# A three-block transformer kernel: forgetting sums apart from the decays, 64 rows a head, and another order of work around the SSD loop

## The reference, cut to what matters

```python
u = rmsnorm(x, norm_mix)
(pool_v, q, k, v, f_logit, z, xbc, dt_raw, gate_logits) = split_columns(u @ w_in)
y_pool = pool_mixer(pool_v, ...) @ p_pool
# forgetting attention, 8 heads of 64
c = cumsum(log_sigmoid(f_logit + f_bias))                 # one row a head
s = q @ k.T * scale + (c[query] - c[key]), causal
y_attn = (softmax(s) @ v) @ p_attn
# SSD, 16 heads of 64, 2 groups, 4 chunks of 128 tokens
xbc = silu(causal_dwconv(xbc)); dt = softplus(dt_raw + bias); a = dt * A
a_cs = cumsum(a) in each chunk
y = (C B^T * exp(a_cs[l] - a_cs[s])) @ (x * dt)  +  exp(a_cs) * C @ state
y = (y + d_skip * x) * silu(z); rms norm in groups of 512 channels, * norm_w
y_ssd = y @ p_ssd
gates = sigmoid(gate_logits)
x = x + (gates[0] * y_pool + gates[1] * y_attn + gates[2] * y_ssd) @ w_out
```

## Time and profile before

| | us |
|---|---|
| median of 3 runs | 2301.11 |
| lowest and highest | 2300.15, 2301.57 |
| the profiled execution | 2300.4 |
| its span on the core | 2298.6 |
| PE busy | 2221.3 (97%) |
| DVE busy | 1391.9 (61%) |
| ACT busy | 795.7 (35%) |
| mean granted clock of PE | 0.988 |

### The profile page before, as it was taken

The page is one execution under the profiler, slowest core; times in us unless marked ns, Lnnn a source line. Parts: engine busy times, 40 slices in busy tenths (PEclk is TensorE's granted clock), DMA queues, the critical chain, the costliest instruction groups (busy, mean ns, idle before and its releaser), DMA issues.

```text
span 2298.6 us, 28503 instructions
## 1 busy us (share of the span) xinstructions
PE 2221.3 (97%) x10128; PEld 1756.8 (76%) x10128; DVE 1391.9 (61%) x2100; ACT 795.7 (35%) x1161; POOL 0.2 (0%) x4
## 2 busy tenths in 40 slices
PE   7999999999999999999999999989899999999998
PEld 5777688888886666788888867777678888888886
DVE  5666654554447776655454475577754557888744
ACT  4445432222225554322222223446622323222222
POOL 0000000000000000000000000000000000000000
PEclk9999999999999999999999999999999999999999
DMA  4111133333331111233333322222223332333332
GB/s 128 55 55 55 46 92 101 91 100 90 99 96 56 55 55 46 78 96 99 96 96 95 100 66 65 53 59 65 55 81 103 92 98 87 99 100 93 94 101 87
DMA packets 368642, 188.29 MB, mean 82 GB/s; under 512 B 8968, under 2 KB 368313, under 8 KB 368569
## 3 DMA queue, kind: packets, MB, share of 16 engines
q1 hardware_dynamic: 368569, 187.30, 28.5%
HBM read 185.18 MB, written 2.10 MB: 81 GB/s over the span
## 4 chain that ended last, share of the span: by engine, by line
PE 83%; DVE 10%; ACT 4%; issue 3%; DMA 0%; DVEq 0%; SPq 0%; ACTq 0%
PE lin L1548 73%; PE S L1572 1%; DVE dmax L992 1%; PE ob L1603 1%; ACT w_hi L520 1%; PE S L1585 1%; DVE conv L1256 1%; PE ob L1697 1%; DVE w_lo L877 1%; PE S L1811 1%; PE S L1590 1%; PE S L1575 1%; DVE prob L1005 0%; PE ob L1837 0%; DVE q_raw L1014 0%
## 5 line engine op out<-in xcount | busy, mean ns | idle before, releaser
L520 ACT ACTIVATE w_hi<-raw 128x1024 fp32r<-128x1024 f32 x361 | 381.0, 1056 | 825.4 <-PE lin L1548 817.3
L877 DVE TENSOR_TENSOR w_lo<-raw,w_hi 128x1024 fp32r<-128x1024 f32 x361 | 441.0, 1222 | 207.4 <-ACT w_hi L520 206.5
L1548 PE MATMUL lin<-h_hi,w_hi 128*128 128x512 f32 x1928 | 498.1, 400 | 7.4 <-DVE exact L1435 2.8
L1548 PE MATMUL lin<-h_lo,w_hi 128*128 128x512 f32 x1928 | 480.5, 391 | 0.0
L1548 PE MATMUL lin<-h_hi,w_lo 128*128 128x512 f32 x1928 | 478.3, 390 | 0.0
L1548 PEld LDWEIGHTS lin<-h_hi,w_hi 128*128 128x128 f32 x1928 | 362.3, 190 | 95.4 <-issue 14.1
L1548 PEld LDWEIGHTS lin<-h_hi,w_lo 128*128 128x128 f32 x1928 | 360.9, 188 | 74.8 <-issue 0.5
L1548 PEld LDWEIGHTS lin<-h_lo,w_hi 128*128 128x128 f32 x1928 | 360.2, 188 | 74.8 <-issue 0.8
L1548 PE MATMUL lin<-gu_lo,w_hi 128*128 128x512 f32 x528 | 131.4, 389 | 0.0
L1548 PE MATMUL lin<-gu_hi,w_lo 128*128 128x512 f32 x528 | 131.4, 389 | 0.0
L1548 PE MATMUL lin<-gu_hi,w_hi 128*128 128x512 f32 x528 | 131.4, 389 | 0.0
(11 more groups left out here) (311 smaller groups left out, 2241.8 us busy)
## 6 DMA issues: line engine op xcount, KB each, us to landing
raw<-in_w_in_dram SPq DMA_DIRECT2D x108, 512.0 KB, 3.8
raw<-in_w_gate_dram SPq DMA_DIRECT2D x44, 512.0 KB, 3.7
raw<-in_w_up_dram SPq DMA_DIRECT2D x44, 512.0 KB, 3.8
raw<-in_ffn_up_dram SPq DMA_DIRECT2D x44, 512.0 KB, 3.8
raw<-in_w_down_dram SPq DMA_DIRECT2D x32, 512.0 KB, 3.8
raw<-in_w_out_dram SPq DMA_DIRECT2D x24, 512.0 KB, 3.8
raw<-in_ffn_down_dram SPq DMA_DIRECT2D x16, 512.0 KB, 3.9
raw<-in_w_down_dram SPq DMA_DIRECT2D x16, 384.0 KB, 3.3
```

The source lines that it names most:

```text
L520: act.activation(w_hi[u.slot][:, :, :], raw[u.slot][:, :, :], ACT.Copy).then_inc(hi_ready, 1)
L877: dve.tensor_tensor(w_lo[u.slot][:, :, :], raw[u.slot][:, :, :], w_hi[u.slot][:, :, :].bitcast(f32), ALU.subtract).then_inc(lo_ready, 1)
L1548: ins = pe.matmul(acc, (wh, wh, wl)[part][:, k, :], (hi, lo, hi)[part][:, k0 + k, :], start=first and part == 0 and k == 0, stop=last and ...
```

## The change

The tile c_plus and c_minus give way to c_fox and c_ssd. c_fox holds the forgetting sums of the 8 heads twice, on rows 0 to 7 (remainder on 32 to 39) and on 64 to 71 (remainder on 96 to 103); c_ssd the 16 chunk sums in the same way. The table pick chooses a head's two rows in either half and has columns with -1 for the keys. So each of two heads uses matmuls of 64 rows, in its own half of the array.

The steps are put in another order: the forgetting sums come first and the scores wait for them alone (FD_FOX = 11, FD_SUMS = 17, FD_ALL = 22). The dt sums follow on DVE in head pair 0, ACT's decays after its roundings there, the transposes to tokens after weigh(0). ACT rounds the first x unit before the third silu. The first x is convolved before the second B group is copied. x_tokens comes ahead of z_tile. On PE the decay matmuls and the first part of a projection come before the states. The first merge gate is taken out before the last y and its sigmoid made then. For tiles 4 to 7 ys_hi is written by ACT, with `scaled` working in place in y_raw, and the last projection of the first merge tile starts on ys_hi before ys_lo is ready. Steps on DVE that aren't shown are moved without a change.

```diff
-        "pick": k % 64 == q,
+        "pick": 1.0 * (k % 32 == q) - 1.0 * (k % 32 == q - 64),
 # ACT
+            def decays():
                 act.wait_ge(fd_step, FD_SUMS)
                 ...
                     hi(At(u + 3))
+                    if n == 0:
+                        decays()
                     keep(n, 2)
...
-                    if t == 3:
+                    if t == 2:
                         hi(At(U_SSD))
...
                     if n < KT - 1:
                         silu_z(n + 1)
+                    else:
+                        act.wait_ge(evac, V_MRG + 1 + CREDIT)
+                        act.activation(g_sig[1][:, :], m_sum[:, :], ACT.Sigmoid).then_inc(mg_sig, 1)
+                        hi(At(U_MRG + 3))
...
+                        if first and b == 1:
+                            for n in range(4, KT):
+                                act.wait_ge(sd_post, POST_SCALED[n])
+                                act.activation(ys_hi[:, n, :], y_raw[:, n, :], ACT.Copy).then_inc(sd_hi, 1)
 # DVE
+                for r in (0, 64):
+                    s.did(dve.tensor_scalar(c_fox[r:r + 8, :], fd_c[0:8, :], 1.0, None, ALU.mult))
+                    s.settle()
+                    s.did(dve.tensor_tensor(c_fox[r + 32:r + 40, :], fd_c[0:8, :], c_fox[r:r + 8, :].bitcast(f32), ALU.subtract))
+                assert s.n == FD_FOX
...
                     if n < 3:
                         fox_tile(n + 1, 0)
+                    if n == 0:
+                        dt_sums()
                     for i in range(2, NB):
                         maximum(n, i)
...
+                        if n == 0:
+                            dt_decays()
                         split(At(u + 3))
                         fox_tile(n + 1, 2)
                         fox_output(n)
+                    if n == 0:
+                        dt_tokens()
...
                         causal_conv(8 + BC_TILES[3], At(V_BC + 3), At(U_BC + 3), 3)
+                        causal_conv(0, At(V_SSD), At(U_SSD), 4)
                         split(At(U_SSD + 1))
...
+                    if n == KT - 1:
+                        leave(At(V_MRG), At(U_MRG))
+                        dve.tensor_tensor(m_sum[:, :], lin[V_MRG % 2][:, :], rsB[:, :], ALU.mult).then_inc(evac, 1)
                     split(At(U_SSD + 2 * n + 4))
                     if n < KT - 1:
+                        x_tokens(n + 1)
                         z_tile(n + 1)
-                        x_tokens(n + 1)
...
+                    gated(0)
+                    split(u0 + 3)
+                    ...
+                    rounded(0)
+                    rounded(1)
+                    scaled(4)
+                    scaled(5)
+                    gate_of(1)
+                    scaled(6)
+                    scaled(7)
+                    rounded(2)
+                    split(u0 + 4)
+                    gated(1)
+                    rounded(3)
+                    for n in range(4, KT):
+                        remainder(n)
+                    split(u0 + 5)
+                    gate_of(2)
 # PE
+                    half = [(slice(64 * a, 64 * a + 64), 2 * n + a) for a in range(2)]
+                    for a, (r, e) in enumerate(half):
+                        pe.matmul(S2[i % 2][:, a, 0:N], c_fox[r, P * i:N], table_r("pick")[r, e:e + 1].to_broadcast([64, N]),
+                                  start=False, stop=True, skip_group_check=True)
+                    for a, (r, e) in enumerate(half):
+                        pe.matmul(S2[i % 2][:, a, 0:N], table_r("pick")[r, 64 + e:65 + e].to_broadcast([64, P]), c_fox[r, 0:N],
+                                  start=False, stop=True, skip_group_check=True)
                     for a in range(2):
-                        pick = table_r("pick")[:, 2 * n + a:2 * n + a + 1]
-                        pe.matmul(S2[i % 2][:, a, 0:N], c_plus[:, P * i:N], pick.to_broadcast([P, N]), start=False, stop=True,
-                                  skip_group_check=True)
-                        pe.matmul(S2[i % 2][:, a, 0:N], pick.to_broadcast([P, P]), c_minus[:, 0:N], start=False, stop=True,
-                                  skip_group_check=True)
...
-                pe.wait_ge(fd_step, FD_ALL)
+                pe.wait_ge(fd_step, FD_FOX)
...
                     weigh(n)
+                    if n == 0:
+                        turn_decays()
...
+                    for a in range(2):
+                        r, e = slice(64 * a, 64 * a + 64), 2 * n + a
+                        pick = table_r("pick")[r, e:e + 1]
+                        pe.matmul(S[a][:, :], pick.to_broadcast([64, P]), c_ssd[r, :], start=True, stop=True).then_inc(sd_dec, 1)
+                    product(At(U_SSD + 2 * n + 2), At(V_SSD + 2 * n + 2), h_hi, h_lo, parts=(0,))
                     pe.wait_ge(sd_xd, 2 * n + 2)
                     for c in range(3):
                         ins = pe.matmul(S[2][:, P * c:P * c + P], Bt[g][:, c, :], xdd[n % 2][:, c, :], start=True, stop=True)
                     ins.then_inc(sd_st, 1)
-                    for a in range(2):
...
+                        if first and b == 2:
+                            pe.wait_ge(sd_post, POST_HI)
+                            pe.wait_ge(sd_hi, 4)
+                            product(u + 1, v + 1, hi, lo, 0, kts, parts=(0,))
+                            pe.wait_ge(sd_post, POST_ALL)
+                            product(u + 1, v + 1, hi, lo, 0, kts, parts=(1, 2))
```

More of the change, by code:

```diff
@@ L1343, in ssd, with scaled @@
                     s.did(dve.tensor_tensor(y_raw[:, n, :], y_t[:, :], zs[n % 2][:, :], ALU.mult))
-            def normed(n):
-                s = Steps(dve, sd_post, At(4 + 2 * n if n < 4 else 3 * n))
-                s.settle()
-                if n == 0:
+            post = Steps(dve, sd_post, At(4))
+            def scaled(n):
+                dve.wait_ge(sd_grs, 4)
+                post.did(dve.scalar_tensor_tensor(y_raw[:, n, :], y_raw[:, n, :], vec[:, R_SNORM + n:R_SNORM + n + 1], grs[1][:, :],
+                                                  ALU.mult, ALU.mult))
+                assert post.start.of(1, post.n) == POST_SCALED[n]
@@ new lines, in rounded, with remainder, merge, begin @@
+            def rounded(n):
+                post.did(dve.tensor_copy(ys_hi[:, n, :], y_raw[:, n, :]))
+                post.settle()
+                post.did(dve.tensor_tensor(ys_lo[:, n, :], y_raw[:, n, :], ys_hi[:, n, :].bitcast(f32), ALU.subtract))
+            def remainder(n):
+                dve.wait_ge(sd_hi, n - 3)
+                post.did(dve.tensor_tensor(ys_lo[:, n, :], y_raw[:, n, :], ys_hi[:, n, :].bitcast(f32), ALU.subtract))
+            def merge():
+                def begin():
+                    s = Steps(dve, mg_step, At(1))
+                    v0, u0 = At(V_MRG), At(U_MRG)
+                    def gated(b):
+                        v = v0 + 2 * b
+                        leave(v + 1, u0 + (2 * b + 1))
+                        dve.wait_ge(mg_sig, b + 1)
+                        dst = m_sum if b == 0 else g_sig[b % 2]
+                        if b == 0:
+                            s.settle()
+                        dve.tensor_tensor(dst[:, :], lin[(v + 1).slot][:, :], g_sig[1 if b == 0 else b % 2][:, :], ALU.mult)\
+                           .then_inc(evac, 1)
+                        dve.wait_ge(evac, (v + 1).of(1, LIN0))
+                        if b:
+                            s.did(dve.tensor_tensor(m_sum[:, :], m_sum[:, :], g_sig[b % 2][:, :], ALU.add))
+                            s.settle()
+                    def gate_of(b):
+                        v = v0 + 2 * b
+                        leave(v, u0 + 2 * b)
+                        dve.tensor_tensor(g_raw[b % 2][:, :], lin[v.slot][:, :], rsB[:, :], ALU.mult).then_inc(evac, 1)
+                    gated(0)
+                    split(u0 + 3)
@@ L1360, in normed @@
-                s.settle()
-                s.did(dve.tensor_tensor(ys_lo[:, n, :], y_n, ys_hi[:, n, :].bitcast(f32), ALU.subtract))
-            def merge():
-                def one(f, last, post=(), first=False):
+                    post.settle()
+                    rounded(0)
[6 more added lines that the diff above has]
+                    rounded(2)
@@ new lines, in begin @@
+                    split(u0 + 4)
+                    gated(1)
+                    rounded(3)
+                    assert post.start.of(1, post.n) == POST_HI + 1
+                    for n in range(4, KT):
+                        remainder(n)
+                    assert post.start.of(1, post.n) == POST_ALL
+                    split(u0 + 5)
+                    gate_of(2)
+                    split(u0 + 6)
+                    gated(2)
+                    split(u0 + 7)
+                    s.did(dve.tensor_scalar(m_hi[:, 0, :], m_sum[:, :], 1.0, None, ALU.mult))
@@ L1365, in one @@
+                    s.settle()
```

(15 more changed lines are left out.)

83 lines of the change are left out of this document (42 added, 41 removed).

## The result

| | before | changed | forecast for the changed kernel |
|---|---|---|---|
| median, us | 2301.22 (4 runs) | 2267.3 (4 runs) | 2268.6 |
| lowest and highest | 2300.15, 2301.57 | 2261.88, 2269.47 | 2265.0 to 2276.5 |
| profiled execution, its span | 2300.4, 2298.6 | 2269.5, 2267.7 | |
| stretch S (below) | 310.28 | 276.08 | 277.1 to 277.8 |

The ratio is 0.9854, with an interval of 0.9838 to 0.987: 33.9 us less, where 32.5 were forecast. The median also lies in the forecast's own, narrower range of 2266.5 to 2271. The page of the changed kernel shows, against the earlier trace rows, that PE works 13.2 us less, while the span is 30.9 shorter: 17.7 of the gain is time in which PE no longer stands still.

What follows compares the result with a forecast made beforehand. TensorE (PE) was taken as the bound, busy 2221.3 of 2298.6 us. Terms 7.0 + 4.0 + 6.1 + 0.3 + 15.8 - 0.7 = 32.5 off the profiled 2300.4 gave 2267.9, plus 0.7 for the median 2268.6; range 2265 to 2276.5.

Steps and rivals of the forecast that it cites:

- sums and decays split: First scores: waiting for the forgetting sums alone, they start earlier and at full clock, less later transposes; 7.0 us gained.
- 64 rows in the scores: Score tiles: sum matmuls of two heads overlap on different array halves, short tiles less; 4.0 us gained.
- first x, and the loop: SSD loop: second x convolution starts 6.1 us earlier, set by DVE; turns then save only 0.3 in all.
- first merge tile: First merge tile: stalls for gate 0, w_hi and ys_lo go, with the half clock there; 15.8 us gained.
- half clock at the last y: Last y: PE idles some 2 us and may then run at half clock, 1.5 lost; half taken, -0.7 us.
- (e): Rival at the first scores: the split changes nothing, scores wait for something else; 7.0 us gone, 2275.6, chance 0.03.
- (a): Rival in the scores: 64-row matmuls in one pass don't overlap; the 4.0 us goes, 2272.6, chance 0.13.
- (d): Rival in scores and SSD: each 64-row sum matmul drains the array; slower than before, 2306 at 0.42 each, chance 0.02.
- Margins: Moved dt sums in head pair 0: DVE finishes what PE needs at turn(0,2) 0.4 to 0.7 us ahead.
- (b): Rival: dt sums late at turn(0,2), ys chain late, and a half-clock window; 4.3 us lost, 2273, chance 0.13.
- (c): Rival: PE's saving counts in the SSD loop, 2 us more, and full score overlap, 2 more; 2264.6, chance 0.07.
- the ring: SSD loop: a chain over DVE and ACT, 15.3 us, as long as the turn, so PE's savings there buy nothing.

Runs made afterwards that it cites:

- wait_all: Changed kernel with the dt sums, decays, transposes and copies back ahead of the first scores, 64 rows kept; median 2275.0 us, ratio 0.9883.
- rows128: Changed kernel with every matmul against the sums on all 128 rows, in scores and SSD loop; median 2269.8 us, ratio 0.9868.
- ys_dve: Changed kernel with ys_hi of tiles 4 to 7 cast on DVE and the ys projection waiting for the last remainder; median 2273.3 us, ratio 0.988.
- first_x: Changed kernel with the first x as before: weights rounded ahead of the fourth silu, convolution after the second B group; median 2270.2 us, ratio 0.9874.
- after_again: The changed kernel run again as it is; median 2266.2 us, ratio 0.9852.
- dt_late: Changed kernel with four more one-input DVE operations, 1.81 us together, in the moved dt sums; median 2271.1 us, ratio 0.9879.

## Why the prediction was right, point by point

| step | forecast | measured |
|---|---|---|
| sums and decays split | 7.0 | 6.9 |
| 64 rows in the scores | 4.0 | 5.2 |
| first x, and the loop | 6.1 + 0.3 | 6.3 |
| first merge tile | 15.8 | 15.8 |
| half clock at the last y | -0.7 | 0 |
| sum | 32.5 | 34.2 |

The measured column is read from the landmarks of both traces, each step up to where its stretch ends; the first two are parted by the tiles' own lengths. The sum is 1.7 off, and two terms make it: 1.2 in the scores and 0.7 for half clock that didn't come.

- **Split.** Up to the first fill projection 8.24 is gained, of which 0.5 is the shorter tiles; 0.83 goes back to the transposes. The scores start 5.33 earlier (5.4 forecast), with the forgetting sums ready 3.4 before PE arrives (3.5 forecast). wait_all gives 6.45 for undoing it. Rival (e) is out.
- **64 rows.** This term was mis-sized. It was taken down to 4.0 since short tiles were thought to overlap less; measured are 0.44, 0.34, 0.24 and 0.26 a tile, with what follows 1.28 to 1.33 a pair of heads, and rows128 gives 5.2. The short ones overlap as well. Rivals (a) and (d) are out.
- **First x.** The second convolution starts 6.07 earlier once the gain before it is taken off, as forecast (6.1), and DVE, which comes to it without an idle, sets it.
- **Loop.** Turns of 15.42 and a wait of 2.1 before the last y were both forecast. What failed is the prediction's "PE idle near 0.4 in each": it is 0.13. The 0.25 that a decay pair was to save on PE isn't saved, either. The pair takes 0.44 on 64 rows (1538.48 to 1538.92) against 0.56 in rows128, but the projection part behind it takes 1.95 against 1.82, so what is saved is given back. The Trainium skill (TensorEngine Tiling (Array Packing), Key Properties) says that a change of tiling mode drains TensorE; the trace agrees in direction, with 0.13 more behind the pair, though no run parts a drain from other fixed costs there. A score tile goes once from 64 rows to 128, before and after, so its 0.44 isn't touched by this.
- **Merge tile.** 15.8 as summed, with the remainders 0.2 ahead of PE where the sum said "just met". Of this 6.2 is shown by ys_dve; how the rest parts into gate 0 and w_hi is argued from the earlier trace rows.
- **Half clock.** Of the eight kernels that idle about 2 us before the last y, two were slowed behind it, at 1.2 or 1.3 each. Half a chance of 1.5 was more than these bear out; the changed kernel's trace has none, and a single trace is luck either way.
- **Margins.** The forecast said 0.4 to 0.7, and turn(0,2) is met by 0.35; but turn(0,3), reached some 0.6 later, is not. Rival (b) decided nothing, but was nearer than it looked. (c) held only for part of its second half: the scores gave 1.2 more than 4.0, where it had 2.

What the prediction doesn't name is the stall at the first norm group's scale, in turn 4 of the loop (n counts from 0). The kernel before stood twice there, and the changed one stands once for as long:

```profile
1600.84 0.66 PE L1905 MATMUL misc<-tab,xs 128*128 128x128 f32 x4 [1.55 <-ACT xs L748]
...
1604.84 0.94 PE L1913 MATMUL S<-xdd,Bt 128*128 128x128 f32 x6 [1.67 <-DVE xdd L1296]
```
```profile
1585.68 0.66 PE L1998 MATMUL misc<-tab,xs 128*128 128x128 f32 x4 [3.13 <-ACT xs L753]
```

Since it is part of the ring that had been counted through to the last y, the sum was right without it.

## What to carry to other kernels

When an engine is late in a loop, follow the ring through all engines to the end of the loop, and count a gain there and not in the turn: PE had gained 8 us by the seventh y_sq sum here, and 6.3 were left at the last y. A ring shorter than PE's work catches up with a late step, one that is longer, here by 0.14, carries it on: an edit that took 0.14 off each turn was worth 5.3. Where executions differ in untouched code, compare a stretch between two landmarks.

## What the runs showed of the hardware

- A stall has a second price, and not always. After 3.38 of idle before the ys parts PE ran at 1.2 GHz and lost 2.83 more; after about 2 before the last y the clock fell in two kernels and stayed in six. After the 3.1 for xs in turn 4 it fell in five of the seven kernels that have that stall (all but the changed one and first_x); by the next y_sq sum they had lost 1.4 to 2.8. Where it was up to 1.6, the later waits for the ring gave nearly all of it back by the last y (after_again, rows128, dt_late); of 2.7 and 2.8, in wait_all and ys_dve, 1.2 and 1.3 stayed. The window of wait_all (clock 0.51):

```profile
1589.00:1596.00 7.00, 5.95 (x37) 4.69 (x38) 4.46 (x6) 2.66 (x5) 0.00 (x0) 0.51 0.29 76
```

- The same program met different stretches of half clock in untouched blocks: 6.2 us between two traces of the changed kernel, nearly all from the clock. That exceeds most of what single edits did here.
- Matmuls on different halves of the rows overlap down to 128 columns: such a score tile went from 1.23 to 0.97. In tiles of 512 the sum matmuls start 0.56 after fq's when they use its halves, and 1.06 after when they need all rows.
